# Loading the output projection's weights during the recurrence, and placing its first two tiles between the last tile's steps

## The reference

```python
def step(state, inp):                      # RWKV-7, one token, per head
    r_t, w_t, k_t, v_t, kk_t, b_t = inp
    sa = jnp.einsum("bhvk,bhk->bhv", state, -kk_t)
    state = (state * w_t[:, :, None, :] + sa[..., None] * b_t[:, :, None, :]
             + v_t[..., None] * k_t[:, :, None, :])
    y_t = jnp.einsum("bhvk,bhk->bhv", state, r_t)
    return state, y_t
...
y = jnp.concatenate([y_a * silu(g_a), y_b * silu(g_b), y_c * silu(g_c)], axis=-1)
out = jnp.einsum("bse,ed->bsd", y, w_out[l])
x = _layer_norm(ALPHA * x.astype(jnp.float32) + out, ln_g[l], ln_b[l]).astype(x.dtype)
```

## Time and profile before

| | us |
|---|---|
| median of 3 runs | 2346.74 |
| lowest, highest | 2341.55, 2349.51 |
| profiled execution | 2345.09 |
| its span | 2343.3 |
| PE busy | 2118.2 (90%) |
| DVE busy | 826.4 (35%) |
| ACT busy | 560.0 (24%) |
| POOL busy | 198.8 (8%) |

### The profile page before, as it was taken

One profiled execution on the slowest core, in us unless ns is written; L12 is line 12 of the kernel. 1 busy time (PEld: TensorE's weight loads), 2 busy tenths in 40 slices (PEclk: granted clock), 3 DMA queues, 4 the chain that ended last, 5 costly groups with the idle time before them and its releaser, 6 DMA issues. The chain is left out here.

```text
span 2343.3 us, 27331 instructions
## 1 busy us (share of the span) xinstructions
PE 2118.2 (90%) x10876; PEld 1221.1 (52%) x10876; DVE 826.4 (35%) x1833; ACT 560.0 (24%) x1349; POOL 198.8 (8%) x297
## 2 busy tenths in 40 slices
PE   8999999786998759999995999999999849999991
PEld 4545554686437534444443657767764324444440
DVE  1116548764154342111114534434431141111115
ACT  1013225332013201111212433333321101111112
POOL 0000002011252100000002000000000000000003
PEclk9999999898998869999997999999999959999996
DMA  3500000000211159999964000000100157999966
GB/s 126 215 23 36 19 2 3 3 4 21 102 42 68 64 241 343 373 417 366 370 269 147 27 1 1 1 1 1 72 13 27 45 239 298 367 368 367 367 271 243
DMA packets 46199, 349.30 MB, mean 149 GB/s; under 512 B 6256, under 2 KB 6576, under 8 KB 36208
## 3 DMA queue, kind: packets, MB, share of 16 engines
q1 hardware_dynamic: 32176, 296.97, 32.4%
q0 software_dynamic: 13888, 50.47, 6.1%
HBM read 292.82 MB, written 54.59 MB: 148 GB/s over the span
## 5 line engine op out<-in xcount | busy, mean ns | idle before, releaser
L202 PE MATMUL psum<-arena 128*128 128x512 f32 (+7 forms) x9328 | 1962.0, 385 | 125.6 <-DVE arena L1906 25.9
L202 PEld LDWEIGHTS psum<-arena 128*128 128x128 f32 (+3 forms) x9328 | 1050.3, 170 | 967.7 <-issue 840.2
L2037 DVE TENSOR_TENSOR arena<-psum,arena 128x256 f32<-128x256 f32 x64 | 27.2, 425 | 541.5 <-ACT arena L2081 541.5
L2117 POOL DMA_INDIRECT arena<-xn_rows,arena x64 | 60.2, 941 | 820.4 <-PE psum L2004 589.6
L2081 ACT ACTIVATE arena<-psum 128x256 f32<-128x256 f32 x64 | 24.7, 385 | 402.3 <-PE psum L202 402.3
L1458 ACT ACTIVATE arena<-arena 128x1024 f32<-128x1024 f32 x43 | 45.4, 1056 | 259.8 <-DVE arena L2772 101.6
L2685 ACT ACTIVATE arena<-psum,arena 128x1024 f32<-128x1024 f32 (+8 forms) x72 | 50.3, 700 | 188.6 <-DVE arena L2721 188.6
L2074 ACT ACTIVATE arena<-psum 128x512 f32<-128x512 f32 x64 | 38.3, 598 | 185.5 <-PE psum L202 185.5
L2004 PE MATMUL psum<-arena 128*128 128x128 f32 x512 | 68.2, 277 | 10.6 <-DMA arena<-xn_rows,arena 10.6
L1176 ACT ACTIVATE arena<-psum 128x256 f32<-128x256 f32 (+3 forms) x128 | 45.7, 369 | 90.7 <-PE psum L202 80.6
L2104 DVE COPY arena<-psum 128x512 f32<-128x512 f32 x64 | 44.3, 692 | 61.4 <-PE psum L202 61.4
(11 more groups left out here) (286 smaller groups left out, 1287.6 us busy)
## 6 DMA issues: line engine op xcount, KB each, us to landing
arena<-in_w_exp SPq DMA_DIRECT2D x64, 3072.0 KB, 12.1
expert_rows<-arena SPq DMA_DIRECT2D x80, 512.0 KB, 3.8
arena<-in_x SPq DMA_DIRECT2D x16, 512.0 KB, 5.1
xn_rows<-arena SPq DMA_DIRECT2D x16, 512.0 KB, 2.6
arena<-in_w_out SPq DMA_DIRECT2D x8, 512.0 KB, 7.0
arena<-in_w_o SPq DMA_DIRECT2D x1, 4096.0 KB, 12.1
out<-arena SPq DMA_DIRECT2D x8, 512.0 KB, 5.8
arena<-in_rows SPq DMA_DIRECT2D x6, 512.0 KB, 6.7
```

The source lines that it names most:

```text
L202: return e.matmul(out, lhsT, rhs, start=start, stop=stop, skip_group_check=True)
L2117: e.indirect_dma_start(out=xe, out_offset=None, in_=xn_dram[:, :], in_offset=bass.IndirectOffsetOnAxis(idx.bitcast(I32)[:, block:block + 1 ...
```

## The change

`wo1` moves to an address that is free once the gated linear recurrence has ended: `xT` takes the place of `w_bufs` at `h_at`, and `w_bufs`, `wo1` and the temporaries of that recurrence share `w_at`. SP gets `sp_rwkv`: it waits for `lru_v` to be 2 (the second L867 on DVE, in the middle of the second tile's rounds) and loads `w_out` there.

The projection's 128 products are now numbered tile by tile, half by half, slice by slice (`OUT1`). Products 0 to 31 (tiles 0 and 1) are issued in `pe_rwkv`, four behind each of the last tile's steps 10 to 17, into banks 0 to 3, which the front has left. The other 96 follow in `pe_out1` behind a wait for ring `bk_`. DVE, ACT and POOL keep their order. SP loads the first two tiles of `x` ahead of the two rows and the meta rows.

```diff
+        wo1 = arena[:, w_at:w_at + KD * D].rearrange("p (a b) -> p a b", a=KD)
+        m_wo1 = [d_row[k].nth() for k in range(KD)]
+        o1 = Banks(banks, *fr.rest(), [((i, hf), "V") for i in range(NT) for hf in range(2)])
+        OUT1 = [(i, hf, k) for i in range(NT) for hf in range(2) for k in range(KD)]
+        TAIL = {s: range(4 * (s - 10), 4 * (s - 9)) for s in range(10, 18)}
+
+        def pe_out1_pass(e, n):
+            i, hf, k = OUT1[n]
+            key = (i, hf)
+            if k == 0:
+                if hf == 0:
+                    e.wait_ge(*tile_out.at(i + 1))
+                wait_all(e, o1.free(key))
+            m = mm(e, o1.bank[key], yT[:, k, P * i:P * (i + 1)], wo1[:, k, half_cols(hf)], k == 0, k == KD - 1)
+            if k == KD - 1:
+                m.then_inc(*o1.fill(key))
+
+        def sp_rwkv(e):
+            e.wait_ge(*lru_v.at(2))
+            for k in range(KD):
+                e.dma_start(wo1[:, k, :], io["w_out"][:, k, :]).then_inc(d_row[k].sem, 16)
...
+                if i == NT - 1 and s in TAIL:
+                    if s == 10:
+                        e.wait_ge(*lru_v.at(2))
+                        wait_all(e, m_wo1)
+                        wait_all(e, fr.totals)
+                    for n in TAIL[s]:
+                        pe_out1_pass(e, n)
...
         def sp_out1(e):
             wait_all(e, after_rwkv)
-            for k in range(KD):
-                e.dma_start(wo1[:, k, :], io["w_out"][:, k, :]).then_inc(d_row[k].sem, 16)
-            e.dma_start(lng, io["rows"][0:1, :].to_broadcast([P, D])).then_inc(d_ln.sem, 16)
-            e.dma_start(lnb, io["rows"][1:2, :].to_broadcast([P, D])).then_inc(d_ln.sem, 16)
-            e.wait_ge(*h_zero.at(1))
-            e.dma_start(h[0:N_META, NT, :], io["meta"]).then_inc(d_meta.sem, 16)
             for i in range(NT):
                 if i >= 2:
                     e.wait_ge(*o1.empty((i - 2, 1)))
                 e.dma_start(xr[i % 2], io["x"][P * i:P * (i + 1), :]).then_inc(d_xr[i % 2].sem, 16)
+                if i == 1:
+                    e.dma_start(lng, io["rows"][0:1, :].to_broadcast([P, D])).then_inc(d_ln.sem, 16)
+                    e.dma_start(lnb, io["rows"][1:2, :].to_broadcast([P, D])).then_inc(d_ln.sem, 16)
+                    e.wait_ge(*h_zero.at(1))
+                    e.dma_start(h[0:N_META, NT, :], io["meta"]).then_inc(d_meta.sem, 16)
 
         def pe_out1(e):
-            wait_all(e, after_rwkv)
-            for g in range(0, NT, 4):
-                steps = [(k, j) for k in range(KD) for j in range(4)] if g == 0 else [(k, j) for j in range(4) for k in range(KD)]
...
+            for n in range(TAIL[17].stop, len(OUT1)):
+                if n == TAIL[17].stop:
+                    wait_all(e, bk_.totals)
+                pe_out1_pass(e, n)
```

More of the change, by code:

```diff
@@ L255, in build @@
         top[0] = h_at
+        xT = take(KD, T)
+        top[0] = w_at = h_at + NS * D
         w_bufs = [take(KD, 512) for _ in range(2)]
-        top[0] = h_at + NS * D
-        xT = take(KD, T)
         yT = take(KD, T)
@@ L280, in build @@
         v_tok = take(NT, P)
-        sig = [arena[:, o:o + 512] for o in (h_at + 2 * KD * 512, h_at + 2 * KD * 512 + 512)]
-        assert h_at + 2 * KD * 512 + 1024 <= base_b1 - 2 * KD * T
+        sig = [arena[:, o:o + 512] for o in (h_at + KD * T, h_at + KD * T + 512)]
+        assert h_at + KD * T + 1024 <= w_at
         proj = [("q", P * j, P, half, "q", j) for half in range(2) for j in range(4)]
@@ L668, in build @@
         yb = Lc
-        top[0] = h_at
+        top[0] = w_at
         lru_t = take(2, T)
-        assert top[0] >= h_at + KD * 256
-        top[0] = h_at + KD * 256
+        assert top[0] >= w_at + KD * 256
+        top[0] = w_at + KD * 256
         xc = take(2, T)
-        assert top[0] <= h_at + KD * 512
-        top[0] = h_at + KD * 512
+        assert top[0] <= w_at + KD * 512
+        top[0] = w_at + KD * 512
         ra, ib = take(2, T), take(2, T)
-        assert top[0] <= h_at + 2 * KD * 512
+        assert top[0] <= w_at + 2 * KD * 512
         base_xb = base_wa + T + 2
@@ L928, in build @@
         Kf, Rf, Vf = [R[2], R[3]], [R[0], R[1]], [R[4], R[5]]
-        areas = [[base_tmp, ARENA], [base_b1 - 2 * KD * T, base_b1 - KD * T]]
+        areas = [[base_tmp, ARENA], [h_at, h_at + KD * T]]
         def take_dead(*dims):
@@ L1336, in build @@
         top[0] = base_b1
-        wo1 = take(KD, D)
         lng, lnb = take(D), take(D)
@@ L1351, in build @@
         d_ln, d_meta = landed("ln"), landed("meta")
-        m_wo1 = [d_row[k].nth() for k in range(KD)]
         m_ln = [d_ln.nth() for _ in range(2)][-1]
@@ L1355, in build @@
         m_xr = [d_xr[i % 2].nth() for i in range(NT)]
-        o1 = Banks(banks, *fr.rest(), [((i, hf), "V") for i in range(NT) for hf in range(2)])
         var_in, dev_in, normal, scaled_by, squared, h_zero = (signal("ln_" + n) for n in
@@ L1410, in sp_out1 @@
                 e.dma_start(xr[i % 2], io["x"][P * i:P * (i + 1), :]).then_inc(d_xr[i % 2].sem, 16)
-        def pe_out1(e):
-            wait_all(e, after_rwkv)
-            for g in range(0, NT, 4):
-                steps = [(k, j) for k in range(KD) for j in range(4)] if g == 0 else [(k, j) for j in range(4) for k in range(KD)]
[L1416 to L1425, removed]
+                if i == 1:
[3 more added lines that the diff above has]
+                    e.dma_start(h[0:N_META, NT, :], io["meta"]).then_inc(d_meta.sem, 16)
+        def pe_out1(e):
+            for n in range(TAIL[17].stop, len(OUT1)):
+                if n == TAIL[17].stop:
+                    wait_all(e, bk_.totals)
+                pe_out1_pass(e, n)
         def dve_out1(e):
@@ L2945, in _ @@
             sp_prep(e)
+            sp_rwkv(e)
             sp_out1(e)
```

## The result

| | before | after |
|---|---|---|
| median, us | 2346.74 | 2327.86 |
| lowest to highest (5 runs each) | 2341.55 to 2349.51 | 2324.0 to 2329.87 |
| profiled execution's span | 2343.3 | 2326.1 |

The ratio is 0.9928, 95% interval 0.9913 to 0.9942: 18.9 us faster by the medians. The trace lies between: the next stage's first product on PE starts at 692.51 us, 15.2 us earlier than before (707.68).

A forecast was written before the change was run, and what follows sets the result against it. PE bounds the stage's end, full behind 585.77 us. Last product: 561.32 + 5.7 + 2.6 + 27.5 + 0.6 + 82.6 = 680.3 against 697.31, 17.0 us earlier, 17.5 with the last tile's 0.5; forecast 2328.5 us, range 2320 to 2338.

The forecast's parts named there:

- The groups cover the gaps: Last tile's steps 10 to 18: groups of four (3.4 us) outlast gaps up to 1.05 us; 0.6 us stays behind step 18.
- Size of the products: Output projection on PE: 0.86 us a product, 27.5 us for the 32 that move, 82.6 for the 96 that stay.
- The recurrence's own products and the changes of shape: PE after step 10: 5.7 us (4.0 to 9.6) for own products, 2.6 us (0 to 6.8) for thirteen shape changes.
- The row I priced them by: Dense stretch of PE at full clock before the change: 259 small records took 9.74 us, 0.0376 each.
- The clock: PE from step 10 through the projection: full clock, 1.00 throughout, with no gap over 0.6 us.
- The loads of w_out at nothing: 4 MB loaded beside the recurrence, landed by some 465 us: slows PE by 0, bound less than 0.1 us.
- DVE and POOL stay covered: Projection's start: DVE comes to tile 0 at 618.4 and returns bank 0 at 619.1, 6 us before PE needs it.
- The end of the stage: Tile 7 goes half by half, so DVE's second read starts at once after PE's end: 0.5 us gained.
- the rivals: Other outcomes: shape changes dear 0.11, DVE holding up PE 0.04, PE's clock falling 0.03, nothing gained 0.04.
- The dear changes of shape: Steps 10 to 18: a drain fences each group, small groups take as long as before; gain 9 to 10 us, 2336; 0.11.
- DVE's wall: Tile 4 of the projection: bank 0 returns late and PE stops; bands at twice 15.7 us give 2338 us; chance 0.04.

The follow-up runs named there:

- the extra changes: Changed kernel with the projection products of steps 11 and 16 put one by one between the steps' own products, 12 more changes of shape; 2328.33 us.
- the second trace: The changed kernel run again word for word, on one chip with a variant that spreads the w_out loads; 2330.34 us, ratio 0.9939 to before.
- the early load alone: Changed kernel with only the early load of w_out kept, all 128 projection products behind step 18; 2339.32 us, ratio 0.9979 to before.

## Why the prediction was right, and where it was not

The forecast was 2328.5 us, the median 2327.86. The mechanism was the forecast one: with the loads early and four products behind each step PE has no gap, and its clock stays up. By its steps:

- *The groups cover the gaps.* Right: no gap from step 10 to step 18, and half as many products cover them too. Behind step 18 the wait was 0.77 us for 0.6.
- *Size of the products.* Right: 82.64 us for the 96 against 82.6.
- *The recurrence's own products and the changes of shape.* Forecast 5.7 + 2.6 = 8.3 us; measured 35.10 less step 10's own 0.68 and less 27.5, 6.9 us. The price of a change was right at 0.20 us, as the extra changes showed. So, at that price for the thirteen changes, it was the small products that were over-sized: 6.9 - 2.6 = 4.3 us for 5.7. The row I priced them by the earlier trace rows, 0.038 us a record, is probably not as dense as groups whose operands are all waiting. No run tests that.
- *The clock.* Right: 1.00 in both stretches.
- *The loads of w_out at nothing.* Wrong, and the largest error: 3.4 us (3.9 in the second trace), by the stop of 2.33 us and the lower clock behind it. I compared turns of the window attention with and without transfers. But those transfers were a share of 0.27, not 1, and PE had 98 records in a turn of 20.3 us; the recurrence has 2742 in 107.6, five times as many for each microsecond. The row bore on the volume and not on full transfer engines beside an engine that eats instructions fast.
- *DVE and POOL stay covered.* Right: 6 us to spare forecast, 6.4 found, and one for one beyond it. They came at 620.4 for 618.4, since the recurrence ended later.
- *The end of the stage.* Right: 0.5 us.

In the trace's terms the forecast was 17.5 us, and it became 15.2: 1.2 us more than forecast from step 10 to the last product (18.2 for 17.0), and 3.4 less ahead of it. The medians gave 18.9 on one occasion and 12.9 on another, so that the first hits the forecast to a microsecond is partly luck: two errors in the trace's terms, 1.2 us one way and 3.4 the other, and the spread of the runs cover each other. None of the rivals came true. The dear changes of shape were tested and are out. DVE's wall exists, but 6.4 us away. The clock fell for 3 us where no rival had it, in the burst's wake.

## What to carry to other kernels

A chain of small steps over several engines is covered as soon as the work placed between them outlasts the longest answer; here two products of 0.86 us did what four did, and the work costs its own time plus 0.2 us for each change of shape. Work that such a move makes early (here the loads) has a price at its new place: find the stretch where the receiving engine issues most instructions and keep full-width bursts out of it, or cut them up (worth 2.5 to 3 us here by the traces, and not told apart by the whole time). And before moving a load next to a condition, look up when that condition becomes true in the trace, not in the order of the code.

## What the runs showed of the hardware that I had not expected

A burst of eight 512 KB loads in a row (383 GB/s and the transfer engines 0.96 busy just ahead of the stop) stopped PE for 2.0 to 2.6 us in all eight traces in which it ran beside the small products, seven at one place and one at another. At the first place the stop fell at the burst's end, at the other in the middle of it. In seven of the eight the clock then fell to 0.50 for some 3 us; behind the shortest stop, 2.05 us in the trace of the early load alone, it stayed at 1.00.

Waits of PE marked "issue", of 0.2 to 1.3 us, also stand where no load runs, in the trace of before too. Their length changes from run to run, down to nothing. Their possible places are fixed in PE's order of work, about 124.4 matmul records or a multiple of it apart, and each ends 1.2 to 1.6 us behind the landing of a 16 KB packet of instructions. Between the third tile's transposes and step 10 they sum to 2.2 us before, and to 4.5 us in the changed kernel.
